# Attention of a hybrid decoder layer: splits ahead of the projection's end, sample keys one unit ahead, three score banks in the second half, output products begun at once

## What is computed

```python
def mem_kv(mem, g_mem, w_mem_k, w_mem_v):
    m = rmsnorm(mem, g_mem)
    k = (m @ w_mem_k).reshape(b, N_MEM, MEM_HEADS, MEM_HD)      # 256 memory rows, 4 heads of 256
    v = (m @ w_mem_v).reshape(b, N_MEM, MEM_HEADS, MEM_HD)
    return k, v

def cross_attn(h, k, v, w_xq, w_xo):
    b, t, _ = h.shape
    q = (h @ w_xq).reshape(b, t, MEM_HEADS, MEM_HD)
    s = jnp.einsum('bthd,bmhd->bhtm', q, k).astype(jnp.float32) * (MEM_HD ** -0.5)
    p = jax.nn.softmax(s, axis=-1).astype(v.dtype)
    o = jnp.einsum('bhtm,bmhd->bthd', p, v).reshape(b, t, D_MODEL)
    return o @ w_xo

def layer(x, k_mem, v_mem, ...):
    x = x + 0.5 * swiglu(rmsnorm(x, g_ffn1), w1_gate, w1_up, w1_down)
    mix, new_pool, new_conv, new_ssm = token_mix(rmsnorm(x, g_mix), ...)
    x = x + mix
    x = x + cross_attn(rmsnorm(x, g_xq), k_mem, v_mem, w_xq, w_xo)
    x = x + 0.5 * swiglu(rmsnorm(x, g_ffn2), w2_gate, w2_up, w2_down)
    return x, ...
...
        hp, pb, cb, sb = layer(hp, k_p, v_p, zero_pool, zero_conv, zero_ssm, 0, lw)              # prompt
        hs, pb2, cb2, sb2 = layer(hs, cache_mem_k[l], cache_mem_v[l], state_pool[l], ...)        # samples
```

## Time and profile before

| | us |
|---|---|
| median of the runs (2225.78 to 2226.51, n = 3) | 2226.3 |
| the profiled execution, on the device | 2226.93 |
| its span | 2225.2 |
| PE busy | 2183.6 |
| DVE, ACT, POOL busy | 1380.0, 700.6, 331.6 |
| stage from the query projection's end to the output projection's start | 105.24 |

### The profile page before, as it was taken

One profiled execution on the slowest core, in us unless ns is written; L12 is line 12 of the kernel. 1 busy time (PEld: TensorE's weight loads), 2 busy tenths in 40 slices (PEclk: granted clock), 3 DMA queues, 4 the chain that ended last, 5 costly groups with the idle time before them and its releaser, 6 DMA issues.

```text
span 2225.2 us, 40853 instructions
## 1 busy us (share of the span) xinstructions
PE 2183.6 (98%) x15968; PEld 2133.8 (96%) x15968; DVE 1380.0 (62%) x2526; ACT 700.6 (31%) x1134; POOL 331.6 (15%) x335
## 2 busy tenths in 40 slices
PE   8999999999999999999999998999999999999998
PEld 8999999999999999987899987899999999999998
DVE  6865555646667775466868345258765555466665
ACT  6332232222123332246714145124323222221124
POOL 2010100123221000024300000000111010133230
PEclk9999999999999999999999999999999999999999
DMA  7231231243223221057724333422223123153222
GB/s 234 68 110 57 69 102 57 91 170 112 105 77 129 71 59 40 21 175 254 214 76 127 122 114 133 155 90 77 90 62 109 57 75 97 58 208 113 79 77 79
DMA packets 222577, 234.37 MB, mean 105 GB/s; under 512 B 8979, under 2 KB 179745, under 8 KB 222201
## 3 DMA queue, kind: packets, MB, share of 16 engines
q1 hardware_dynamic: 222465, 232.83, 32.2%
HBM read 180.42 MB, written 52.48 MB: 105 GB/s over the span
## 4 chain that ended last, share of the span: by engine, by line
PE 57%; DVE 4%; ACT 2%; issue 1%; DMA 0%; DVEq 0%; SPq 0%; ACTq 0%
PE bank L3097 18%; PE bank L3098 18%; PE bank L3099 18%; ACT kTs L1798 1%; DVE dec L2608 1%; DVE cea L2620 1%; ACT pr L1790 1%; DVE w_lo L1907 0%; PE bank L3812 0%; DMA out_mem_k_prompt_dram<-kst 0%; PE bank L3890 0%; ACT h_hi L1781 0%; PE bank L3824 0%; ACT dec L1667 0%; DVE xs L2628 0%
## 5 line engine op out<-in xcount | busy, mean ns | idle before, releaser
L3097 PE MATMUL bank<-h_hi,w_hi 128*128 128x352 f32 (+1 forms) x3392 | 1049.9, 310 | 3.5 <-DVE h_lo L2989 2.7
L3098 PE MATMUL bank<-h_lo,w_hi 128*128 128x352 f32 (+1 forms) x3392 | 1041.3, 307 | 0.0
L3099 PE MATMUL bank<-h_hi,w_lo 128*128 128x352 f32 (+1 forms) x3392 | 1041.1, 307 | 0.0
L3097 PEld LDWEIGHTS bank<-h_hi,w_hi 128*128 128x128 f32 x3392 | 638.2, 188 | 5.2 <-DVE h_lo L2989 3.0
L3098 PEld LDWEIGHTS bank<-h_lo,w_hi 128*128 128x128 f32 x3392 | 639.0, 188 | 0.0
L3099 PEld LDWEIGHTS bank<-h_hi,w_lo 128*128 128x128 f32 x3392 | 637.8, 188 | 0.0
L2247 DVE SCALAR_TENSOR_TENSOR x<-bank,x 128x352 f32<-128x352 f32 x448 | 227.4, 521 | 130.6 <-PE bank L3099 129.8
L3098 PE MATMUL bank<-xr,w_hi 128*128 128x264 f32 x640 | 181.8, 284 | 0.0
L3097 PE MATMUL bank<-xr,w_hi 128*128 128x264 f32 x640 | 181.5, 284 | 0.1
L3099 PE MATMUL bank<-xr,w_lo 128*128 128x264 f32 x640 | 181.5, 284 | 0.0
L1049 POOL TENSOR_TENSOR act<-p,act 128x264 f32<-128x264 f32 x40 | 38.2, 954 | 817.2 <-DVE p L2120 817.2
(11 more groups left out here) (446 smaller groups left out, 2942.2 us busy)
## 6 DMA issues: line engine op xcount, KB each, us to landing
act_keep<-act SPq DMA_DIRECT2D x88, 264.0 KB, 2.0
w_raw<-in_w_gate_dram SPq DMA_DIRECT2D x44, 512.0 KB, 5.2
w_raw<-in_w_up_dram SPq DMA_DIRECT2D x44, 512.0 KB, 3.8
w_raw<-in_w_down_dram SPq DMA_DIRECT2D x44, 512.0 KB, 3.5
h_raw<-act_keep SPq DMA_DIRECT2D x24, 528.0 KB, 4.5
l_raw<-act_keep SPq DMA_DIRECT2D x20, 528.0 KB, 5.4
w_raw<-in_w_in_dram SPq DMA_DIRECT2D x18, 512.0 KB, 4.2
x<-x_keep SPq DMA_DIRECT2D x6, 1408.0 KB, 10.6
```

Source lines behind the costliest of these rows:

```text
L3097: eng.matmul(out, a_hi, b_hi, start=first, stop=False, skip_group_check=onto)
L3098: eng.matmul(out, a_hi, b_lo, start=False, stop=False, skip_group_check=onto)
L3099: return eng.matmul(out, a_lo, b_hi, start=False, stop=last, skip_group_check=onto)
```

## The change

The splits of keys and values are made in halves (`ka`, `va`, `kb`, `vb`): ACT makes the first two after product 99, the others after product 100; on DVE all low parts move up by one to three evictions, so that none is left behind the last eviction. Scores 0 and 1 wait for the 23rd and 24th eviction instead of both for the 24th. A sample's keys are turned and copied in the unit before that in which its scores are made; the lists of PE and ACT are reordered for it. ACT's `att_o` moves ahead of the exponentials; DVE's `att_max` moves behind `att_lo` in units 0 to 7. From unit 7 on, scores are made three units ahead, with bank 6, which no keys need any more, as a third bank. The sample softmax moves up by a unit, and the sample values are spread one by one over units 9 to 15 (two in unit 14) ahead of the unit's values. ACT splits the weights 2 and 3 of the output projection in units 13 and 14. The output projection waits only for the splits of unit 14; those of unit 15 and of the samples are waited for at its ninth product, and the turns of `o_s` stand behind its first. Nothing of the computation is added or left out. SP's and POOL's lists are the same.

```diff
--- before.py
+++ after.py
@@ -61,11 +61,11 @@
...
-S_SOFT, S_SCALE, S_BACK, S_VALUES, S_OUT = 8, 9, 10, 11, 15
+V_UNIT = (9, 10, 11, 12, 13, 14, 14, 15)
 HEADS_AT = (0, 3, 1, 2)
...
 N_SPLIT = 66
-SPLIT = ("q0", "q1", "q2", "q3", "q4", "k", "v", "q5", "q6", "q7")
+SPLIT = ("q0", "q1", "q2", "q3", "q4", "ka", "va", "kb", "vb", "q5", "q6", "q7")
@@ -458,6 +458,10 @@
...
+        def score_bank(u):
...
+            return bank[u % 2] if u < NB else bank[(0, 1, 6)[(u - NB) % 3]]
@@ -1763,10 +1767,12 @@
...
                 q_hi(t)
-            eng.wait_ge(p_ready, 100)
             eng.wait_ge(s_rows, 48)
-            eng.activation(kT_hi[:, :, :], kT[:, :, :], ACT.Copy).then_inc(n_hi, 1)
-            eng.activation(v_hi[:, :, :], v[:, :, :], ACT.Copy).then_inc(n_hi, 1)
+            for half in range(2):
+                eng.wait_ge(p_ready, 99 + half)
+                kd = slice(4 * half, 4 * half + 4)
+                eng.activation(kT_hi[:, kd, :], kT[:, kd, :], ACT.Copy).then_inc(n_hi, 1)
+                eng.activation(v_hi[:, half, :], v[:, half, :], ACT.Copy).then_inc(n_hi, 1)
@@ -1787,7 +1793,7 @@
...
                     c_ = 2 * (u % 2) + j
-                    eng.activation(pr[c_][:, :], bank[u % 2][:, 256 * j:256 * j + 256], ACT.Exp, bias=amax[:, c_:c_ + 1],
+                    eng.activation(pr[c_][:, :], score_bank(u)[:, 256 * j:256 * j + 256], ACT.Exp, bias=amax[:, c_:c_ + 1],
                                    scale=ATT_SCALE, accum_out=amax[:, 4 + c_:5 + c_]).then_inc(a_e, 1)
@@ -1798,40 +1804,45 @@
...
+            take_key(0, 0)
+            take_key(0, 1)
             att_exp(0)
+            take_key(0, 2)
+            take_key(0, 3)
+            att_exp(1)
             att_turned(0)
-            att_exp(1)
...
             for u in range(NU):
-                if u < NB:
-                    take_key(u, 0)
-                    take_key(u, 1)
-                if u + 2 < NU:
-                    att_exp(u + 2)
                 if u >= 1:
                     att_o(u - 1)
-                if u + 1 < NU:
-                    att_turned(u + 1)
-                if u < NB:
-                    take_key(u, 2)
-                    take_key(u, 3)
-                if u in (2, 4, 6):
-                    q_hi(4 + u // 2)
-                if u == S_SOFT:
+                if u in (1, 3, 5):
+                    q_hi(5 + u // 2)
+                if u + 1 < NB:
+                    take_key(u + 1, 0)
+                    take_key(u + 1, 1)
+                    att_exp(u + 2)
+                elif u + 2 < NU:
+                    att_exp(u + 2)
+                if u == NB - 1:
                     eng.wait_ge(b_d, 1)
...
                                    accum_out=amax[:, 11:12]).then_inc(b_e, 1)
-                if u == NU - 1:
+                if u + 1 < NU:
+                    att_turned(u + 1)
+                if u + 1 < NB:
+                    take_key(u + 1, 2)
+                    take_key(u + 1, 3)
+                if u in (NU - 3, NU - 2):
                     eng.wait_ge(a_s, NU)
-                    hi_unit(U_XO, 2, 0)
-                    eng.wait_ge(b_v, NB)
-                    eng.activation(o_s[:, :], bank[3][:, 0:MHD], ACT.Copy).then_inc(b_o, 1)
+                    hi_unit(U_XO, u + 5 - NU, 0)
+            eng.wait_ge(b_v, NB)
+            eng.activation(o_s[:, :], bank[3][:, 0:MHD], ACT.Copy).then_inc(b_o, 1)
             att_o(NU - 1)
...
             ins.then_inc(a_oh, 1)
-            hi_unit(U_XO, 3, 0)
             for pair in range(2):
@@ -2885,20 +2896,25 @@
...
                 eng.wait_ge(n_hi, split_done(what))
-                eng.tensor_tensor(out[:, :, :], src[:, :, :], hi[:, :, :].bitcast(F32), ALU.subtract).then_inc(n_lo, 1)
...
+                eng.tensor_tensor(out, src, hi.bitcast(F32), ALU.subtract).then_inc(n_lo, 1)
...
+            kd = (slice(0, 4), slice(4, 8))
             for nq in range(8, 24):
...
                     q_lo(nq - 16)
-                if nq in (20, 21):
-                    q_lo(nq - 18)
-                if nq == 22:
+                if nq == 19:
+                    q_lo(2)
+                    q_lo(3)
+                if nq == 20:
                     q_lo(4)
-                    row_lo("k", kT_lo, kT, kT_hi)
-            row_lo("v", v_lo, v, v_hi)
+                    row_lo("ka", kT_lo[:, kd[0], :], kT[:, kd[0], :], kT_hi[:, kd[0], :])
+                    row_lo("va", v_lo[:, 0, :], v[:, 0, :], v_hi[:, 0, :])
+                if nq == 21:
+                    row_lo("kb", kT_lo[:, kd[1], :], kT[:, kd[1], :], kT_hi[:, kd[1], :])
+                    row_lo("vb", v_lo[:, 1, :], v[:, 1, :], v_hi[:, 1, :])
@@ -2947,7 +2963,7 @@
...
                 eng.wait_ge(a_s, u + 1)
-                link(eng.tensor_reduce(m_, bank[u % 2][:, :].rearrange("p (t m) -> p t m", t=2), AX.X, ALU.max))
+                link(eng.tensor_reduce(m_, score_bank(u)[:, :].rearrange("p (t m) -> p t m", t=2), AX.X, ALU.max))
                 link(eng.tensor_scalar(m_, m_, -ATT_SCALE, None, ALU.mult))
@@ -2963,33 +2979,37 @@
...
             att_max(1)
+            att_scale(1)
             att_turned(0)
-            att_scale(1)
...
             for u in range(NU):
-                if u + 2 < NU:
+                ahead = u + 2 < NU
+                if ahead and u >= NB:
                     att_max(u + 2)
-                if u == S_SOFT:
-                    sample_max()
                 if u >= 1:
                     att_lo(u - 1)
-                if u + 2 < NU:
+                if ahead and u < NB:
+                    att_max(u + 2)
+                if u in (1, 3, 5):
+                    q_lo(5 + u // 2)
+                if u == NB - 1:
+                    sample_max()
+                if ahead:
                     att_scale(u + 2)
...
                     att_turned(u + 1)
-                if u in (2, 4, 6):
-                    q_lo(4 + u // 2)
-                if u == S_SCALE:
+                if u == NB - 1:
                     sample_scale()
-                if u == S_BACK:
+                if u == NB:
                     sample_back()
...
             w_split(U_XO + 2)
+            w_split(U_XO + 3)
             eng.wait_ge(a_oh, NU + 1)
...
             ins.then_inc(a_ol, 1)
-            w_split(U_XO + 3)
             for n in range(NT):
@@ -3728,6 +3748,8 @@
...
                                 eng.wait_ge(w_ready, w + 2)
+                            if last == 4 and (group, n, four) == (0, 2, 0):
+                                eng.wait_ge(a_ol, NU + 1)
                             project(w, n, first if group == 0 and four == 0 else None)
@@ -3743,6 +3765,8 @@
...
                                 norm_spread(last, 0)
+                            if last == 4 and (group, n, four) == (0, 0, 0):
+                                sample_back()
                             if last == 4 and group == 1 and (n, four) in ((1, 2), (2, 2)):
@@ -3752,16 +3776,16 @@
...
-            eng.wait_ge(q_ready, 24)
-            eng.wait_ge(s_rows, 48)
...
             def scores(u):
                 tp, h = unit_at(u)
-                wait(eng, a_e, 2 * (u - 1))
-                eng.wait_ge(n_lo, split_done("k" if tp < 2 else "q5" if tp == 2 else "q7"))
+                if u < 2:
+                    eng.wait_ge(q_ready, 23 + u)
+                else:
+                    eng.wait_ge(a_e, 2 * (u - 1) if u < NB + 3 else 2 * (u - 2))
+                eng.wait_ge(n_lo, split_done("vb" if tp < 2 else "q5" if tp == 2 else "q7"))
                 for j in range(2):
-                    o, tk = bank[u % 2][:, 256 * j:256 * j + 256], slice((2 * tp + j) * P, (2 * tp + j + 1) * P)
+                    o, tk = score_bank(u)[:, 256 * j:256 * j + 256], slice((2 * tp + j) * P, (2 * tp + j + 1) * P)
                     for kd in range(2):
@@ -3783,8 +3807,6 @@
...
                 wait(eng, a_ol, u - 1)
-                if u == 0:
-                    eng.wait_ge(n_lo, split_done("v"))
                 for d_ in range(2):
@@ -3826,36 +3848,56 @@
...
+            def turn_keys(b, two):
...
+                sample_turn(b, 2 * two)
+                sample_turn(b, 2 * two + 1)
...
             scores(0)
+            turn_keys(0, 0)
             scores(1)
+            turn_keys(0, 1)
+            scores(2)
             turn_p(0)
-            for u in range(NU):
-                if u + 2 < NU:
...
+            for u in range(NB):
+                if u:
                     scores(u + 2)
-                if u < NB:
-                    sample_turn(u, 0)
-                    sample_turn(u, 1)
+                sample_scores(u)
+                if u + 1 < NB:
+                    turn_keys(u + 1, 0)
+                turn_p(u + 1)
+                if u + 1 < NB:
+                    turn_keys(u + 1, 1)
+                else:
+                    scores(u + 3)
+                values(u)
+            for u in range(NB, NU):
+                if u + 3 < NU:
+                    scores(u + 3)
```

(29 more changed lines are left out.)

## The result

The changed kernel took 2207.11 us (median of 4 runs, 2206.57 to 2207.32) against 2226.04 for the kernel before in the same comparison: 18.9 us less, a ratio of 0.9915 with an interval of 0.9898 to 0.9933. In two later comparisons it was 2206.85 against 2227.04 and 2206.47 against 2226.24, 20.2 and 19.8 us less. The span of its profiled execution is 2205.6, of that before 2225.2.

What follows compares the result with a forecast made beforehand. TensorE, busy 98% of the span, was taken as the bound, only its waits as gainable. Terms 4.7 + 0.46 + 6.65 + 5.45 + 4.2, less 0.6 and 0.35, gave 20.5; with a recount, 20.7: 2205.6 us, range 2204.2 to 2212.0.

Steps and rivals of the forecast that it cites:

- The ceiling: All PE stall in the stage between query and output projection, 21.8 us, the most any reordering there could gain.
- Part 1: Splits ahead, at the stage's start: gap before scores, wait for turned probabilities and slow clock go, 4.7 us.
- Part 2: Sample keys turned one unit ahead, first half: seven waits of 0.95 us go, 6.65 us; period 6.3.
- The tight spot: PE's fourth key turn in a unit, against ACT's key copies: costs 0.05 us a unit, 0.35 in seven.
- The switches: PE changing between wide and narrow products in the first half: costs 0.08 us a unit, 0.6 in all.
- Part 3: Three score banks, second half: loop of DVE and ACT falls from 4.45 to 3.4 us, waits of 5.45 go.
- Part 4: Output products start at once after the last values: wait of 2.85 us and slow clock go, gain 4.2.
- the recount: The stage's PE work summed by pieces: 85 us instead of 105.24, 20 gained, 21.5 with the clock after it.
- A: Rival: a new wait, on key copies, loop, values block or x reload, replaces the old; gain 13 to 18, chance 0.25.
- B: Rival: most comes back as one chain, or splits aren't ahead; gain 5 to 13 us, chance 0.08.
- D: Rival: no effect, within 4.5 us, because another engine's queue is the bound; chance 0.03.
- C: Rival: slower, the denser stage running at the lower clock level, 2239 us with half its issue there; chance 0.03.

Runs made afterwards that it cites:

- before: The kernel before, unchanged, in its first profiled execution: 2226.93 us, stage 105.24 us.
- before_again: The kernel before, unchanged, profiled once more for its clock: 2225.89 us, stage 104.12 us.
- late_sample_scores: The kernel before with one edit on PE, sample scores of a unit made behind the scores of the next unit: 2218.15 us, stage 95.99 us.
- splits_alone: The kernel before with only the splits in halves and earlier, scores 0 and 1 waiting for evictions 23 and 24: 2224.0 us, stage 102.43 us.
- splits_late: The changed kernel with the splits late again, scores still waiting for the last split, that of the values: 2213.17 us, stage 92.32 us.
- output_waits: The changed kernel with the turns of o_s and the wait for all output splits ahead of the output projection again: 2212.19 us, stage 90.31 us.
- two_banks: The changed kernel with two score banks all through instead of a third in the second half: 2206.13 us, stage 86.08 us.
- after_third: The changed kernel without an edit, run again as a base: 2206.47 us, stage 86.08 us.
- paired_values: The changed kernel with the sample values in pairs in units 11 to 14: 2206.44 us, stage 86.03 us.

## Why the prediction was right, point by point

It forecast 2205.6 in a range of 2204.2 to 2212.0; 2207.1 is in it. The gain was 18.9 where 20.7 was forecast, 19.8 and 20.2 in the other comparisons.

**The ceiling and the stage.** The sum gave a stage of 85.9 (105.24 less the 20.7, without the 1.6 of clock that lies behind it and the 0.25 of `o_s`); it took 86.08, of which PE is drawn busy 85.99, a hair under the 86 that the prediction had set as the mark of being wrong. The 1.5 us between forecast and time lie elsewhere: in the profiled pair the changed kernel came to the stage 0.56 later (1297.45 and 1296.89), well within the scatter told above, and its output projection ran at 0.161 instead of 0.159 us per matmul for a while, some 0.5. The remaining 0.4 fits a clock that costs less in the median than in the one trace from which the sum was made. Only traces show where it falls, but the mean granted clock of each execution is on record: of the 29 executions of the kernel before that stand beside the experiments, six have 0.995 and take 2227.6 us on average, seven have 0.997 and take 2225.8. So taking the clock's 3.1 us in full from one execution is the term that was too large: the 1.5 of it in the stage was there in one of two traces of the same kernel, and cost 1.12 between the two.

**Part 1 was sized wrongly.** 4.7 was given to the splits (0.98 + 2.2 + 1.5). Alone they are worth 1.7 with the clock at 1.00 (2.8 against the trace in which it fell), and taken out of the changed kernel 1.27. The wait for the probabilities was counted as the splits' gain, though the same paragraph had the key turns in front of it, which cover it by themselves. The sum held, since the stall was counted once; its label was wrong. The timing was right: no gap, last split at 1293.5 with PE asking at 1297.45.

**Part 2 was right in kind and size.** 6.65 of waits gone, a period of 6.27 where 6.3 was forecast. The tight spot, the fourth key turn, took nothing that can be seen: the second pair of keys takes 0.88 (1312.65 to 1313.53), as before. The switches are there: 0.09 for narrow products behind scores (0.21 from start to start, less 0.12), and 0.05 for keys behind narrow ones (the first pair takes 0.93, 1311.28 to 1312.21), where 0.10 was forecast. And what I didn't see: sample scores that move into unit 8 fill 1.2 us of the second half's first wait.

**Part 3 had the right loop and the wrong name.** The loop 4.45 was measured again with the old order (4.44), and the order of ACT is what removed it: 2.6 us. The third bank gave the part its heading, and is worth nothing. Of the 5.45 us forecast here, these 2.6 and the 1.2 that the moved sample scores fill have an experiment; the remaining 1.7 or so has none of its own, and scores three units ahead were never undone. The scale and the turn of the sample softmax, by the way, move up by two units, not by one like its maximum; that is what lets sample values begin in unit 9. Missed as well: ACT's output copy, now first, holds the exponentials of unit 15 behind the values of unit 12. The maxima of unit 15 were ready at 1373.38; ACT got to the exponentials at 1374.36; PE came to turn unit 15 after values issued until 1376.73, and waited 0.24 (DVE, then ACT):

```profile
1373.21 0.17 DVE L2967 TENSOR_SCALAR amax<-amax 128x2 f32<-128x2 f32 x1
...
1373.87 0.60 ACT L1787 ACTIVATE h_hi<-bank 128x512 fp32r<-128x512 f32 x1 [2.02 <-PE bank L3119]
1374.36 0.47 ACT L1796 ACTIVATE pr<-bank,amax 128x256 f32<-128x256 f32 x1
```

**Part 4 was right in kind.** Undone it costs 5.4, with the slow clock, where 4.2 was forecast, since PE comes to that wait sooner in the changed kernel and stands for 3.86 instead of 2.73; done, PE passes from values to products without a gap, the turns of `o_s` stand in 0.13 behind product 0, and the first addition is ended by the transfer, as forecast.

**Small slips.** The four waits of the second half are 5.53 from issue to issue, not 5.45; the recount, 105.24 less 85.1, is 20.1 and with the clock 21.7; and a first output product at 1382.3 doesn't fit the sum, which gives 1382.8. None moves the forecast by more than 0.5.

**Rivals.** A (a new wait of 3 us and more) left only the 0.24 above. B and D didn't come. C, the clock in the denser stage: 1.00 throughout. The Trainium skill's account of a kernel that cycles through PSUM banks ("TensorE: Matmul & The Clock Gate", Part 1), weighed in the prediction, isn't borne out in this stage: 1.00 for 86 us with three banks and with two.

## What to carry to other kernels

Where the busiest engine waits for a copy it has just asked for, look for another step of its own list to put in between; one moved step gave 8 of the 19 us here. When stalls overlap, their sum is a sound forecast of all edits together and a bad one of each, so undo each edit in the finished kernel to see what it is worth: the third bank was worth nothing, and the order of two copies 2.6 us. Behind an engine whose list is in order, ask of every step that is moved to the front what it waits for itself.

## What the runs showed of the hardware

The lower clock level behind an idle spell of PE is not certain. Behind 2.1 us idle it came in one of three executions (before; not before_again or late_sample_scores), behind 2.7 us in two of four (before and before_again; not splits_alone or late_sample_scores), behind 3.5 us (splits_late) and 3.9 us (output_waits) in the one trace that each has. Ahead of the stage, every one of the fourteen traces has an idle spell of 2.0 us near 1055, and the lower level follows it in eight:

```profile
1056.09 0.45 PE L3673 MATMUL bank<-xs,dsk 64*64 64x128 f32 x2 [1.98 <-DVEq L2654]
```

```profile
1056.10:1059.50 3.40, 3.40 (x30) 3.07 (x32) 2.81 (x5) 3.37 (x10) 1.47 (x1) 0.51 0.88 351
```

```profile
1054.50:1058.00 3.50, 3.50 (x45) 2.89 (x46) 2.79 (x5) 3.47 (x10) 1.47 (x1) 1.00 0.79 328
```

The first two are of the changed kernel, the third of two_banks. Nor is one long spell needed: in four traces (before, before_again, after_third, splits_late) the level falls near 1104, behind two spells of 0.56 to 0.96 us, while in two_banks the clock stays at 1.00 behind spells of 0.93 and 0.56 there. The cost was 1.1 us by the stages of the two traces of before, 1.5 to 1.7 at the output projection (the rest of traces with and without it, at the same pace of matmuls), and some 2.6 behind the 3.5 us. The Trainium skill ("TensorE: Matmul & The Clock Gate", Part 1) says that the number of slow matmuls at a kernel's start varies from run to run; here it is whether the level falls at all that varies.

At a granted clock of 1.00 the 352-column matmuls of the output projection came every 0.159 us in some executions and every 0.161, easing to 0.160 and 0.159 within some 60 us, in others: before, output_waits, splits_alone and paired_values belong to the first, before_again, all three of the changed kernel and the other six to the second. It is worth under 1 us. What decides it is open.
